# Borders between the stages of a hybrid decoder layer: loads, masks and the out stage's beginning moved

## What is computed

```python
u = rmsnorm(h) @ w_in            # q latent 256 | kv latent 256 | rope key 64 | delta q,k,v 3x512 | z 512 | a 4 | b 4
# MLA group: 4 heads (128 + 64 rope, v 128)
q  = (rmsnorm(q_lat, q_a_norm_w) @ w_q_b)      # per head rmsnorm, rope
kv = (rmsnorm(kv_lat, kv_a_norm_w) @ w_kv_b)   # per head rmsnorm, rope
o_mla = rmsnorm(causal_softmax_attention(q, k, v), mla_out_norm_w)
# DeltaNet group: causal depthwise conv of width 4 + silu, then the gated delta rule in chunks of 64
o_dn = rmsnorm(delta(conv_silu(qkv), decay(a), sigmoid(b)), dn_out_norm_w) * silu(z)
h = h + concat(o_mla, o_dn) @ w_out
h = h + convglu(rmsnorm(h, ffn_norm_w))        # width-3 conv between up-projection and activation
```

## Time and profile before

| | us |
|---|---|
| median of 3 runs | 3245.88 |
| lowest and highest run | 3242.87, 3246.95 |
| the profiled execution | 3256.48 |
| its span in the trace | 3254.8 |

### The profile page before, as it was taken

How to read it: one execution, slowest core, us unless ns; L and a number is a source line. 1 busy time by engine, 2 the same in 40 slices (tenths; PEclk the granted TensorE clock), 3 DMA queues, 4 the chain that set the end, 5 groups by cost and what they waited for, 6 DMA issues and landing times. The chain is left out here.

```text
span 3254.8 us, 49226 instructions
## 1 busy us (share of the span) xinstructions
PE 2873.8 (88%) x19127; PEld 2499.6 (77%) x19127; DVE 1810.0 (56%) x2752; ACT 1186.9 (36%) x2197; POOL 1110.3 (34%) x1195
## 2 busy tenths in 40 slices
PE   6797848996899979999299679999999999699999
PEld 6797748996788868888287568888878888588887
DVE  3123833443355467776579466665697777524444
ACT  3223722221444455554233243333343333323312
POOL 2602740001777500000254255555566666200000
PEclk9998978998799989999699889999999999899999
DMA  6953673223444131210357533223353333545554
GB/s 235 364 168 92 170 235 127 89 75 90 91 107 101 41 109 56 75 56 20 129 169 230 177 127 96 92 93 98 94 173 107 105 97 104 192 125 190 172 169 146
DMA packets 413470, 421.97 MB, mean 130 GB/s; under 512 B 38282, under 2 KB 335766, under 8 KB 412214
## 3 DMA queue, kind: packets, MB, share of 16 engines
q1 hardware_dynamic: 379534, 306.64, 31.2%
q10 hardware_dynamic: 21384, 67.36, 6.3%
q0 software_dynamic: 12320, 44.80, 4.1%
HBM read 258.18 MB, written 160.55 MB: 129 GB/s over the span
## 5 line engine op out<-in xcount | busy, mean ns | idle before, releaser
L2836 PE MATMUL fu_pM<-fu_us_hi,fu_w_hi 128*128 128x512 f32 x1232 | 488.6, 397 | 35.9 <-DVE fu_us_lo L2669 35.9
L2836 PE MATMUL fu_pM<-fu_us_lo,fu_w_hi 128*128 128x512 f32 x1232 | 486.4, 395 | 0.0
L2836 PE MATMUL fu_pM<-fu_us_hi,fu_w_lo 128*128 128x512 f32 x1232 | 486.0, 394 | 0.0
L2836 PEld LDWEIGHTS fu_pM<-fu_us_hi,fu_w_hi 128*128 128x128 f32 x1232 | 235.6, 191 | 88.6 <-issue 29.0
L2836 PEld LDWEIGHTS fu_pM<-fu_us_hi,fu_w_lo 128*128 128x128 f32 x1232 | 235.4, 191 | 50.1
L2836 PEld LDWEIGHTS fu_pM<-fu_us_lo,fu_w_hi 128*128 128x128 f32 x1232 | 235.5, 191 | 48.7
L3071 PE MATMUL fd_pM<-fd_bs_hi,fd_a_hi 128*128 128x512 f32 x616 | 241.5, 392 | 27.6 <-DVE fd_bs_lo L3003 22.4
L3071 PE MATMUL fd_pM<-fd_bs_hi,fd_a_lo 128*128 128x512 f32 x616 | 240.6, 391 | 0.0
L3071 PE MATMUL fd_pM<-fd_bs_lo,fd_a_hi 128*128 128x512 f32 x616 | 240.4, 390 | 0.0
L2583 ACT ACTIVATE fu_w_hi<-fu_sw 128x512 fp32r<-128x512 f32 x176 | 111.3, 633 | 323.6 <-PE fu_pM L2836 262.5
L2998 DVE TENSOR_TENSOR fd_a_lo<-fd_a_lo,fd_a_hi 128x1408 fp32r<-128x1408 f32 x56 | 91.0, 1626 | 235.9 <-ACT fd_a_hi L2954 235.9
(11 more groups left out here) (403 smaller groups left out, 7174.2 us busy)
## 6 DMA issues: line engine op xcount, KB each, us to landing
fd_a_lo<-scr_gs ACTq DMA_DIRECT2D x56, 704.0 KB, 4.6
fu_w_raw<-in_w_gate SPq DMA_DIRECT2D x22, 1024.0 KB, 5.5
fu_w_raw<-in_w_up SPq DMA_DIRECT2D x22, 1024.0 KB, 5.3
scr_gs<-fu_sg SPq DMA_DIRECT2D x88, 256.0 KB, 2.7
scr_gs<-fu_acc SPq DMA_DIRECT2D x66, 256.0 KB, 2.5
pj_wd<-in_w_down POOLq DMA_DIRECT2D x11, 1024.0 KB, 12.0
scr_td<-pj_td POOLq DMA_DIRECT2D x11, 1024.0 KB, 8.6
fd_b_raw<-scr_td SPq DMA_DIRECT2D x44, 256.0 KB, 5.1
```

Of the source, the lines that this page charges most:

```text
L2836: p = pe.matmul(bank(2 * n + m, i)[:, :], a[:, k, :], x[:, k, :], start=(k == 0 and n_pass == 0), stop=(k == HALVES_K - 1 and n_pass == 2))
```

## The change

- The query stage's weights and gains are issued at the end of GpSimd's program in the project stage, behind its last `td` store, and no longer in turn 6 of SP's.
- In the query stage latents are loaded 5 tiles ahead (was 4) in a ring of 6 (was 4) and normed 4 ahead (was 3), on ACT and DVE.
- The last column tile of conv runs taps and silu in two halves, each behind its own raw half.
- Delta's masks are built by GpSimd in the conv stage (`delta_masks`); the scales and decays stay in SBUF from conv to delta; the first tile's `dn_kv` rows are issued by ACT.
- Attention's first queries, the whole first head's keys and values and the meta tokens' are issued by SP in the delta stage, turns 4 to 10 (`load_attention`).
- Four parts of w_out and two gains are issued by GpSimd in attention, behind the fifth output store. The other four parts are loaded at the out stage's start into the last four buffers of `ot_u`. ACT issues one transfer there, not nine.
- The out stage's first two tiles are written out by hand, with the weights' splitting among them, and PE multiplies four of tile 0's eight blocks before it turns tile 1.
- In all out tiles GpSimd multiplies y by its gains first, behind the scaling of the tile before, and z and the gate last; DVE reduces the squares behind the reciprocal.
- `build` opens the shared rooms in one more nest around conv to out.

```diff
-            def load_next(t, s, u):
-                if t == 6:
-                    for of, name in ((slice(0, QW), "w_q_b"), (slice(QW, QW + KVW), "w_kv_b")):
-                        sp.dma_start(S["qw_raw"][:, :, of], A[name][0].rearrange("(k p) n -> p k n", p=P)).then_inc(S["qw_loaded"], 16)
...
-            plain(TILES, (2, lambda t, s, u: load(t, s, u) if t >= 2 else None), (0, store), (-1, store_tok), (0, load_next))
+            plain(TILES, (2, lambda t, s, u: load(t, s, u) if t >= 2 else None), (0, store), (-1, store_tok))
...
+            for of, name in ((slice(0, QW), "w_q_b"), (slice(QW, QW + KVW), "w_kv_b")):
+                pool.dma_start(S["qw_raw"][:, :, of], A[name][0].rearrange("(k p) n -> p k n", p=P)).then_inc(S["qw_loaded"], 16)
+            for n, name in enumerate(("q_a_norm_w", "kv_a_norm_w")):
+                pool.dma_start(S["q_lat_gain"][:, n * LORA:(n + 1) * LORA],
+                               A[name][0:1, :].to_broadcast([P, LORA])).then_inc(S["q_consts"], 16)
+            for n, name in enumerate(("q_norm_w", "k_norm_w")):
+                pool.dma_start(S["q_nope_gain"][:, n:n + 1], A[name][0, 0:NOPE].unsqueeze(1)).then_inc(S["q_consts"], 16)
+                pool.dma_start(S["q_rope_gain"][:, n, :], A[name][0:1, NOPE:QK].to_broadcast([P, ROPE])).then_inc(S["q_consts"], 16)
...
-        KPE_RING = 4
+        KPE_RING = 6
...
-            plain(TILES, (4, load), (0, store_values), (-2, store), (1, load_tables))
+            plain(TILES, (5, load), (0, store_values), (-2, store), (1, load_tables))
...
-            plain(TILES, (0, heads), (2, latents_hi), (0, squares), (-2, out), (0, roots), (3, latents))
+            plain(TILES, (0, heads), (2, latents_hi), (0, squares), (-2, out), (0, roots), (4, latents))
...
-            plain(TILES, (2, latents_lo), (-2, out_nope), (0, heads), (-2, out_rope), (1, rotary_key), (0, scale), (3, latents))
+            plain(TILES, (2, latents_lo), (-2, out_nope), (0, heads), (-2, out_rope), (1, rotary_key), (0, scale), (4, latents))
...
+            delta_masks(r, pool, S)
...
+                if t == MT - 1:
+                    for g in range(NG):
+                        dve.wait_ge(raw_out[g], t + 1)
+                        part = slice(g * CG * N, (g + 1) * CG * N)
+                        for j in range(TAPS):
+                            tap = taps[:, j * MT + column(t):j * MT + column(t) + 1]
+                            shifted = raw[:, j + g * CG * N:j + (g + 1) * CG * N]
+                            if j == 0:
+                                dve.tensor_scalar(acc[:, part], shifted, tap, None, ALU.mult).then_inc(conv_step, 1)
+                            else:
+                                dve.wait_ge(conv_step, (TAPS - 1) * (t + g) + j)
+                                m = dve.scalar_tensor_tensor(out=acc[:, part], in0=shifted, scalar=tap, in1=acc[:, part],
+                                                             op0=ALU.mult, op1=ALU.add)
+                                m.then_inc(conv_step if j < TAPS - 1 else last_part[g], 1)
+                    return
...
+        def load_rows(queue, t):
+            rows = S["dtok"][t * P:t * P + P, :].rearrange("(c t) (e h d) -> h t c e d", c=2, h=2, d=P)
+            for hh in range(2):
+                for c in range(2):
+                    queue.dma_start(kv[t % LOADS][HALVES[hh], c, :, :], rows[hh, :, c]).then_inc(loaded[t % LOADS], 16)
...
+            def load_attention(t, s, u):
+                if t in (4, 5):
+                    n = t - 4
+                    h, g = AT_ORDER[n]
+                    cols = slice(N_META + AT_GW * g, N_META + AT_GW * (g + 1))
+                    sp.dma_start(f(S["at_q_lo"][n][:, :]), S["qT"][h, 0:NOPE, cols]).then_inc(S["at_q_loaded"][n], 16)
+                    for half in HALVES:
+                        sp.dma_start(f(S["at_qr_lo"][n][half, :]), S["qT"][h, NOPE:QK, cols]).then_inc(S["at_q_loaded"][n], 16)
+                if 6 <= t < 6 + AT_GROUPS:
+                    g = t - 6
+                    at, cols = N_META + AT_GW * g, at_key_part(g)
+                    sp.dma_start(f(S["at_k_lo"][:, cols]), S["kT"][0, 0:NOPE, cols]).then_inc(S["at_loaded"]["k"][g], 16)
+                    for half in HALVES:
+                        sp.dma_start(S["at_kr_raw"][half, cols], S["kT"][0, NOPE:QK, cols]).then_inc(S["at_loaded"]["kr"][g], 16)
+                    sp.dma_start(f(S["at_v"][:, AT_QB * g:AT_QB * g + AT_QB, 1, :]),
+                                 S["v"][0, at:at + AT_GW, :].rearrange("(j p) d -> p j d", p=P)).then_inc(S["at_loaded"]["v"][g], 16)
+                if t == 6 + AT_GROUPS:
+                    for n, name in enumerate(("qT", "kT")):
+                        sp.dma_start(S["at_qkm"][:, n, :, :], S[name][:, 0:NOPE, 0:N_META].rearrange("h d t -> d h t")
+                                     ).then_inc(S["at_m_loaded"], 16)
+                        sp.dma_start(S["at_qkm_rope"][:, n, :, :], S[name][:, NOPE:QK, 0:N_META].rearrange("h d t -> d h t")
+                                     ).then_inc(S["at_m_loaded"], 16)
+                    sp.dma_start(S["at_vm_raw"][:, :, :], S["v"][:, 0:N_META, :].rearrange("h p d -> p h d")
+                                 ).then_inc(S["at_m_loaded"], 16)
+
...
-            plain(DT, (LOADS, load), (-1, store(0)), (-1, store(1)))
+            plain(DT, (LOADS, load), (-1, store(0)), (-1, store(1)), (0, load_attention))
...
+            load_rows(act, 0)
...
+                if n == 4:
+                    for k in range(OUT_EARLY):
+                        pool.dma_start(S["wo_raw"][:, k, :], A["w_out"][0, k * P:k * P + P, :]).then_inc(S["wo_loaded"][k], 16)
+                    for i, name in enumerate(("mla_out_norm_w", "dn_out_norm_w")):
+                        pool.dma_start(S["wo_gain"][:, i, :], A[name][0:1, :].to_broadcast([P, VD])).then_inc(S["wo_gains"], 16)
...
+        w_raw = [w_raws[:, i, :] for i in range(OUT_EARLY)] + [
+            u[U_SPARE + i][:, :, :].rearrange("p k n -> p (k n)") for i in range(KD - OUT_EARLY)]
...
+            load(0, 0, 0)
+            load(1, 1, 0)
+            for k in range(OUT_EARLY, KD):
+                sp.dma_start(w_raw[k], A["w_out"][0, k * P:k * P + P, :]).then_inc(w_loaded[k], 16)
+            plain(TILES, (2, lambda t, s, u: load(t, s, u) if t >= 2 else None), (-4, store_joined))
...
             def gate(t, s, u):
+                pool.wait_ge(y_loaded[s], 32 * (u + 1))
+                if t >= 2:
+                    pool.wait_ge(mixed[1 - s], u + s)
+                pool.tensor_tensor(yg[s][:, HEADS:, :], y[s][:, HEADS:, :],
+                                   gain[:, 1:2, :].to_broadcast([P, HEADS, P]), ALU.mult).then_inc(gated, 1)
+                pool.tensor_tensor(yg[s][:, 0:HEADS, :], y[s][:, 0:HEADS, :],
+                                   gain[:, 0:1, :].to_broadcast([P, HEADS, P]), ALU.mult)
                 pool.wait_ge(z_inv[s], u + 1)
-                pool.wait_ge(yg_ready[1 - s], u + s)
+                if t:
+                    pool.wait_ge(yg_ready[1 - s], u + s)
                 pool.tensor_tensor(zg[:, :], z[s][:, :], ez[s][:, :], ALU.mult).then_inc(gated, 1)
-                pool.wait_ge(mixed[s], u)
-                pool.wait_ge(gated, 2 * t + 1)
+                pool.wait_ge(gated, 2 * t + 2)
                 pool.tensor_tensor(yg[s][:, HEADS:, :].rearrange("p h d -> p (h d)"),
-                                   y[s][:, HEADS:, :].rearrange("p h d -> p (h d)"), zg[:, :], ALU.mult).then_inc(gated, 1)
-                pool.tensor_tensor(yg[s][:, 0:HEADS, :], y[s][:, 0:HEADS, :], gain[:, 0:HEADS, :], ALU.mult)
-                pool.wait_ge(gated, 2 * t + 2)
-                pool.tensor_tensor(yg[s][:, HEADS:, :], yg[s][:, HEADS:, :], gain[:, HEADS:, :],
-                                   ALU.mult).then_inc(yg_ready[s], 1)
+                                   yg[s][:, HEADS:, :].rearrange("p h d -> p (h d)"), zg[:, :], ALU.mult).then_inc(yg_ready[s], 1)
 
...
+            weights(0, 1)
+            squares(0, 0, 0)
+            weights(2, 3)
+            roots(0, 0, 0)
+            squares(1, 1, 0)
+            weights(4, 5)
+            hi(0, 0, 0)
+            weights(6, 7)
+            roots(1, 1, 0)
+            plain(TILES, (0, lambda t, s, u: hi(t, s, u) if t else None), (2, norm), (-1, norm2), (-2, u_part))
...
             def norm(t, s, u):
-                dve.wait_ge(squared[s], u + 1)
-                dve.wait_ge(logs[s], u)
-                dve.tensor_reduce(st[s][:, 0, :], sq[s][:, :, :], AX.X, ALU.add).then_inc(summed[s], 1)
                 dve.wait_ge(z_exp[s], u + 1)
                 dve.tensor_scalar(ez[s][:, :], ez[s][:, :], 3e38, 1.0, ALU.min, ALU.add).then_inc(z_one, 1)
                 dve.wait_ge(z_one, t + 1)
                 dve.reciprocal(ez[s][:, :], ez[s][:, :]).then_inc(z_inv[s], 1)
-                if isinstance(t, int) and t == 0:
-                    weights(range(4))
```

(20 more changed lines are left out.)

346 lines of the change are left out of this document (169 added, 177 removed).

## The result

| | median us | lowest, highest | runs |
|---|---|---|---|
| before | 3246.41 | 3242.87, 3249.48 | 4 |
| after | 3172.05 | 3162.82, 3174.71 | 4 |
| after again, as a control | 3163.91 | 3159.79, 3175.08 | 4 |

The ratio to before is 0.9766 (95% interval 0.9743 to 0.9790) in the first series and 0.9747 (0.9715 to 0.9780) in the control, each with its own runs of before on the same chip. The forecast was 3165 us, range 3147 to 3189. The profiled execution of after took 3174.48 us, its span is 3172.8: 82.0 us less than before's, where the sum said 81.

A forecast was written before the change was run, and what follows sets the result against it. Stages run one behind another with PE busy 88%, so the gain lies where PE stands still. Terms of 82.5 us less 1.5 give 81 off 3256.48, 3175.5; less 10.6 to the median, 3165 us, range 3147 to 3189.

The forecast's parts named there:

- Project, 12 us: Project stage: query weights moved to GpSimd shorten PE's longest stop of 17.2 us; 12 us gained, bounds 5 and 16.
- Rival (a): Project stage: PE's stop only moves because DMA engines stay full until 170; gain 3, not 12; 3174 us; chance 0.12.
- Query stage, 12 us: Query stage: earlier latents take 0.9 of 1.28 us off about 14 steady tiles; 12 us, bounds 0 and 16.
- Rival (b): Query tile stays at 8.16 us, ACT and DVE waiting for each other; gain 1, not 12; 3176 us; chance 0.12.
- Conv to delta, 12 us: Delta's start: masks built in conv end ACT's 18.58 us wait, loads then taking 6.6; 12 us, bounds 9 and 14.
- Delta carries the loads, 0 us: Delta: seven tiles carrying some 0.8 MB each of attention's loads on SP's queue cost 0, upper bound 3 us.
- Delta to attention, 5.5 us: Attention's start: rows already in place, ACT 4.7 us sooner, PE between 4.7 and 8; 5.5 us gained.
- Out stage, beginning, 31 us: Out stage's start: DVE waits for no gain, tile 1's multiply ends sooner; 31 us gained, bounds 22 and 36.
- rival (c): Out stage's beginning bound by transfers, late w_out rows holding DVE; 9 us less gain; 3174 us; chance 0.12.
- Gates, 5 us: Out stage's joined tiles: GpSimd's gain products beside DVE's one-input work save PE's waits; 5 us, bounds 0 and 6.
- 1.5 us for the nest of rooms: One more nest opened and closed around the middle stages costs 1.5 us, bounds 0 to 5.
- The conversion to the median: Profiled execution lay 10.6 us over the median of the runs, taken off 3175.5 to give 3164.9.

The follow-up runs named there:

- the kernel in turn 6: The changed kernel with the query stage's weights and gains issued on SP's queue again, in turn 6 of the project stage: 3184.95 us, 0.9806 of before.
- Turn 8 on SP's queue: The changed kernel with the query stage's weights and gains issued on SP's queue, in turn 8 of the project stage: 3176.07 us, 0.9776 of before.
- the combined kernel: The changed kernel with spread two-column products, GpSimd's tile 1 behind tile 0's mix, and tile 0's gate ahead of the first weight rows: 3153.61 us, 0.9713 of before.

## Why the prediction was right, and where not

The whole: 3165 us against 3172.05 and, in the control, 3163.91; 2.5% less was forecast, 2.3 and 2.5 measured. For the profiled execution the sum gave 3175.5 and it took 3174.48. Point by point:

- **Borders pass their gain on.** Right. 82.0 us of span are the sum of the stages' differences, and gate-up and down, which the change leaves alone, took 4.9 of the 87 that the others gave: 1.7 by the clock, some 3 by PE's waits at gate-up's start. That is within what such a stage moves by itself (gate-up 954.1 to 959.2 us with the same program).
- **The sum, right to 1 us: luck.** The single terms missed by +7.1, +5.5 and +1.6 us on one side and by −5.0, −4.2, −3.1 and −2.1 on the other, and these happen to cancel.
- **Project, 12 us: too small**, 19.1 in the profiles, above the upper bound of 16, and 15 by the kernel in turn 6 against the median of eleven. Two steps were off. I took 3 us off for the weights' traffic at 157, but no stop came of it (the two that PE has from 100 us on are 3.9 us together). And I left out that PE runs at the low clock behind a stop, which the row of 160 to 170 (0.81) showed: 1.9 us in these ten. PE's waits went from 20.7 to 3.9 us, 16.8 less, and with the 1.9 that makes 18.7 of the 19.1. Rival (a) is out. The rule quoted from the Trainium skill (DMA: Bandwidth & Descriptors, Issuing engines are not separate DMA queues) says that the issuing engine saves issue time alone. Turn 8 on SP's queue (269.1 us against 259.0 to 269.1) doesn't contradict it, but these weights went out 11 us sooner than GpSimd's, so it is no test of it either.
- **Query stage, 12 us: too small**, 17.5, above the 16 that I used as the bound. I took 0.9 of the 1.28 us, because ACT's wait for DVE's sums would surface. It stayed what it was, beside PE's work. The tile went from 8.16 to 7.04, which is 1.12 in each of some 15. Rival (b) is out, and the kernel with latents three ahead gives back 16.6 us.
- **Conv's halves, 5 us: right**, 5.5.
- **Conv to delta, 12 us: too large**, 9.9. The loads were mis-sized: 6.6 us by the row of attention's start, 10.0 measured. That row's first rows were three transfers; here eight must have landed, which takes 8.5, and 1.5 more beside two other tiles' loads.
- **Delta carries the loads, 0 us: right.** Of the 3.1 us that delta lost 1.5 are the clock's; the other 1.6 lie inside the 308 to 312 that the length less the loss takes in all.
- **Delta to attention, 5.5 us: right**, 5.4; 3 to 6 by the kernel with the loads at attention's start.
- **Out stage, beginning, 31 us: too large**, 26.0. The order of events was right (turn, four blocks, turn, DVE as the bound, no wait for w_out: rival (c) is out). The term mis-sized was DVE's work up to the first turn. The mix begins 16.5 us behind the border where I had 15.5, with a scale of one input at 1.49 us, not 0.42, and itself takes 3.65 beside GpSimd where I had 1.2. The kernel with GpSimd's tile 1 held back gives 2.2 us again (with the variation said there). The one with both edits has its first turn 4.5 us sooner and ends tile 1's multiply at 51.7 us, where 52 was forecast, so what DVE loses beside GpSimd is enough to account for the miss. I had taken one-input instructions as safe beside GpSimd. The Trainium skill (SBUF — State Buffer, Who interferes with whom) names two cases in which VectorE contends with GpSimd: two inputs in SBUF, and an instruction of the kind of a copy or a tensor_scalar in a 2-port perf mode; the trace agrees with the first by the mix (1.21 to 3.65), and with the second in so far as the scale grew beside GpSimd (0.42 to 1.49, and 0.43 in the combined kernel, where GpSimd stands idle then); in which mode it ran no trace shows.
- **Gates, 5 us: somewhat too small, and not a term of its own.** 7.1 us in the joined tiles, above the upper bound of 6. And in the new beginning the old order would cost another 10, which a separate term doesn't show. Had the change come without the new order, I should have been wrong by that much.
- **1.5 us for the nest of rooms.** Not seen: ACT's idle time at the out stage's border is 7.77 us where it was 6.93, so under 1 us there, and no run took the nest away.
- **The conversion to the median** was the weakest step of all. Before's profiled execution lay 10 us above its median, after's 2.4. I took the 10 off as if they belonged to the kernel. The executions of one kernel differ by up to 20 us (before, 3239.46 to 3259.34), with delta's falls of the clock (9.1 to 17.2 us) as one part of it that I found, and that is the noise of the whole forecast.

## What to carry to other kernels

Where stages stand one behind another, look at the borders first, each with its own list of what is late: what an idle engine or queue can do in the stage before is worth its time up to the next thing that is late (here 9.9 of the 18.6 us that the masks took, since then the rows were late). When two edits meet in one stage's beginning, write the order of instructions out and walk through it with both, since the sum of the two terms can be wrong by more than either. An instruction's length is taken from a row with the same neighbours: beside GpSimd an instruction of DVE can take three times as long.

## What was not expected of the hardware

The granted clock of a PE that has no gap falls from 1.00 to 0.50 (2.4 and 1.2 GHz) when a group of 32 two-column instructions holds it for 3.6 us, and stays there for 3.4 or 6.8 us, with six of ten groups in these three profiles (six or seven in others), not the same ones in each execution. This costs 14 to 15 us in a stage of 955. With two such products at a time between products of 512 columns it doesn't fall there, and with fourteen of sixteen left out it doesn't either. This is the largest gain that the runs found behind the change itself, and no view of waits shows it, since PE counts as busy all the time; the column PEclk does.
